# Moving the second tile's hybrid input projection ahead of the first expert gathers

## The reference, cut to what matters

```
h   = rms_norm(x, attn_norm)                     # h0, h1 for tile 0, 1
p   = h @ hyb_w_in                               # 1024 x 2760: the hybrid input projection
q,k,iq,ik of p are rotated (rope), iw picks keys, v stays
x  += attention(...) @ hyb_w_out                 # 16 heads: 8 with top-k selected keys, 8 plain
h   = rms_norm(x, ffn_norm)
q   = h @ w_q  (1024 x 2048)                     # then scores against 128 sub-keys, top 16 of each half,
expert, g = top-16 of the sums per head          # 8 heads, 16 experts each, chosen per token
x  += sum_k g_k * gelu(h . u_tab[expert_k]) * v_tab[expert_k]
```

## Time and profile before

| | us |
|---|---|
| median of 3 runs | 2119.39 (2116.23 to 2121.25) |
| the profiled execution's own time | 2126.27 |
| its span (first to last instruction) | 2124.5 |
| first gather starts (span time) | 560.49 |
| HBM read | 718.66 MB |

### The profile page before, as it was taken

The page is one execution under the profiler, slowest core; times in us unless marked ns, Lnnn a source line. Parts: engine busy times, 40 slices in busy tenths (PEclk is TensorE's granted clock), DMA queues, the critical chain, the costliest instruction groups (busy, mean ns, idle before and its releaser), DMA issues.

```text
span 2124.5 us, 15629 instructions
## 1 busy us (share of the span) xinstructions
PE 1621.2 (76%) x4546; PEld 816.7 (38%) x4546; DVE 1394.3 (66%) x3285; ACT 382.0 (18%) x886; POOL 1136.0 (53%) x1028
## 2 busy tenths in 40 slices
PE   3997999998555868988786788878668896566555
PEld 1465888444222434433343333334334442111111
DVE  6654342142798586588757668776684887777775
ACT  1022000012111022222222222221222221100001
POOL 0000000000376667677767767777687677777773
PEclk9976999998777979999897899999889999866888
DMA  9851468162699999999999999999999999999997
GB/s 357 294 200 60 159 198 325 54 240 79 235 370 327 401 397 387 402 404 408 401 401 401 405 403 405 406 376 402 397 367 379 406 397 369 407 410 409 409 409 311
DMA packets 254482, 720.78 MB, mean 339 GB/s; under 512 B 24518, under 2 KB 49598, under 8 KB 253886
## 3 DMA queue, kind: packets, MB, share of 16 engines
q0 software_dynamic: 147456, 536.94, 64.6%
q1 hardware_dynamic: 106942, 182.85, 24.0%
HBM read 718.66 MB, written 1.05 MB: 339 GB/s over the span
## 4 chain that ended last, share of the span: by engine, by line
PE 40%; DMA 22%; POOL 16%; DVE 12%; issue 7%; ACT 2%; SPq 1%; POOLq 0%; DVEq 0%; ACTq 0%
POOL gring L1699 16%; DMA gring<-in_peer_v_dram,sel_idx 15%; PE PS L621 12%; PE PS L753 7%; PE PS L825 5%; PE PS L826 5%; DMA gring<-in_peer_u_dram,sel_idx 4%; PE PS L727 4%; DVE gring L1537 3%; PE PS L566 3%; DMA wring<-in_hyb_w_in_dram 2%; DVE xs L1556 1%; PE PS L670 1%; PE PS L687 1%; PE PS L706 1%
## 5 line engine op out<-in xcount | busy, mean ns | idle before, releaser
L1699 POOL DMA_INDIRECT gring<-in_peer_u_dram,sel_idx x512 | 574.7, 1123 | 731.6 <-DVE sel_g L1523 560.0
L825 PE MATMUL PS<-gring,diags 128*128 128x512 f32 x704 | 426.6, 691 | 345.3 <-DMA gring<-in_peer_v_dram,sel_idx 217.3
L1699 POOL DMA_INDIRECT gring<-in_peer_v_dram,sel_idx x512 | 561.0, 1096 | 229.7 <-issue 126.7
L1537 DVE CUSTOM_DVE_ANT_0 gring<-gring,hs 128x1024 f32<-128x1024 f32 x400 | 482.5, 1222 | 142.9 <-DMA gring<-in_peer_u_dram,sel_idx 141.5
L621 PE MATMUL PS<-wring,hTs 128*128 128x512 f32 (+3 forms) x968 | 415.4, 580 | 20.2 <-DVE hTs L1125 8.3
L826 PE MATMUL PS<-gring,diags 128*128 128x512 f32 x704 | 413.5, 673 | 0.0
L825 PEld LDWEIGHTS PS<-gring,diags 128*128 128x128 f32 x704 | 126.7, 207 | 564.0 <-issue 412.5
L621 PEld LDWEIGHTS PS<-wring,hTs 128*128 128x128 f32 x968 | 180.8, 197 | 233.5 <-issue 226.0
L826 PEld LDWEIGHTS PS<-gring,diags 128*128 128x128 f32 x704 | 151.6, 215 | 199.2 <-issue 199.2
L1063 ACT ACTIVATE diags<-consts,acts 128x128 f32<-128x128 f32 x352 | 129.7, 396 | 482.4 <-PE PS L826 447.0
L1537 DVE CUSTOM_DVE_ANT_0 gring<-gring,PS 128x1024 f32<-128x1024 f32 x112 | 136.5, 1221 | 70.7 <-DMA gring<-in_peer_u_dram,sel_idx 70.7
(11 more groups left out here) (194 smaller groups left out, 1167.8 us busy)
## 6 DMA issues: line engine op xcount, KB each, us to landing
wring<-in_peer_w_q_dram SPq DMA_DIRECT2D x32, 1024.0 KB, 14.2
wring<-in_w_ada_dram SPq DMA_DIRECT2D x24, 1024.0 KB, 9.7
wring<-in_w_up_dram SPq DMA_DIRECT2D x44, 512.0 KB, 5.0
wring<-in_hyb_w_in_dram SPq DMA_DIRECT2D x20, 1024.0 KB, 7.8
wring<-in_w_in_dram SPq DMA_DIRECT2D x10, 1024.0 KB, 8.5
wring<-in_hyb_w_out_dram SPq DMA_DIRECT2D x8, 1024.0 KB, 21.5
gring<-in_peer_u_dram,sel_idx POOLq DMA_INDIRECT x512, 13.1
gring<-in_peer_v_dram,sel_idx POOLq DMA_INDIRECT x512, 13.6
```

Of the source, the lines that this page charges most:

```text
L825: pe.e.matmul(ybank[0], d, row[i % NG][:, 0:512], start=first, stop=last)
L1537: e.tensor_tensor_reduce(row[i % NG], row[i % NG], hbank if (l, t) == (1, 1) and hd else h[t], 1.0, 0.0, ALU.mult, ALU.add, acts[:, c:c + ...
L1699: gp.e.indirect_dma_start(out=row[i % NG], out_offset=None, in_=table, in_offset=bass.IndirectOffsetOnAxis(ap=sel_idx[:, c:c + 1], axis=0) ...
```

## The change

The end of tile 1's first block (`sq g1`, `norm g1`, `add g1`) and the norm of tile 1's h (`sq h1`, `norm h1`) move to just behind the first step of tile 0's `hyo`. h1's transposes are put behind the first step of `c00`; their result is written back into `h[1]` itself (in place), not into `hT`, and is the left operand of the projection. The seven column groups of `hyi` for tile 1 are put as follows: group 0 before the norm of `c00`; groups 1 to 4 behind pick parts 0 to 3 of group g = 0 (between the two `wq` steps of g = 1); group 5 behind pick part 4; group 6 behind `qturn` of g = 1 and the first `wq` step of g = 2. All seven are read out of PSUM by ScalarE as plain copies, the first six into `ahead`, a part of `keep`, and are not rotated there. The rotation is six new steps `hrope` on VectorE at the head of `hybrid(1)`, each counted as 1.5 units. `PACE[0]` becomes 251.4.

```diff
-PACE = (296.0, 216.3, 243.3)
+PACE = (251.4, 216.3, 243.3)
     def hybrid(t):
         if t:
-            put("sq", "h1")
-            yield 1.0
-            put("norm", "h1")
-        yield 3.0
-        put("hT", f"h{t}")
-        yield 1.0
-        put("hTe", f"h{t}")
-        yield 1.0
-        yield from projection(("hyi", t), (t,))
+            for c in range(6):
+                put("hrope", c)
+                yield 1.5
+        else:
+            put("hT", "h0")
+            put("hTe", "h0")
+            yield from projection(("hyi", 0), (0,))
         put("hqk", t)
...
+        if steps[-1] == ("mm", ("hyo", 0), (0,), 0, 0, 0):
+            put("sq", "g1")
+            put("norm", "g1")
+            put("add", "g1")
+            put("sq", "h1")
+            put("norm", "h1")
+
+    def hyi_ahead():
+        for c in range(7):
+            for k0 in (0, 4):
+                put("mm", ("hyi", 1), (1,), c, k0, 1)
+                if k0:
+                    put("evac", ("hyi", 1), c, 1)
+                yield
+
+    ahead = hyi_ahead()
     c00 = choose(0, 0)
-    while ("pick", 0, 0, 0, 5) not in steps:
+    next(c00)
+    put("hT", "h1")
+    put("hTe", "h1")
+    for _ in range(2):
+        next(ahead)
+    while ("qturn", 0, 0, 0) not in steps:
         next(c00)
-    put("sq", "g1")
-    while ("pick", 0, 0, 0, 6) not in steps:
+    while ("qturn", 0, 0, 1) not in steps:
         next(c00)
-    put("norm", "g1")
-    put("add", "g1")
+        if steps[-1][0] == "pick" and steps[-1][4] < 5:
+            for _ in zip(range(2), ahead):
+                pass
+    for _ in ahead:
+        pass
     together(16 + 32 * 7, PACE[0], c00, hybrid(1), choose(1, 0))
...
+        ahead = keep[:, 2816:5376]
...
-                        take(("mm", name, c, tl), "act" if name[0] == "wq" else "vec" if name[0] in (
+                        take(("mm", name, c, tl), "act" if name[0] == "wq" or name == ("hyi", 1) else "vec" if name[0] in (
...
+                if name[0] == "hyi" and c < 6:
+                    at, w = SPOTS[c0]
+                    last = copy(ahead[:, at:at + w], ps[:, 0:w])
+                    if c0 in (512, 1152):
+                        last = copy(val(t, 8) if c0 == 512 else iw[t], ps[:, 64:n])
+                    freed(key, last)
+                    return
...
+                    dst = hT[:, i0:i0 + 4, 0:128]
+                    if key == ("hT", "h1"):
+                        dst = h[1][:, 128 * i0:128 * i0 + 512].rearrange("p (b q) -> p b q", q=128)
...
+            def hrope(c):
+                c0 = PROJ["hyi"][1][c][0]
+                at, w = SPOTS[c0]
+                there(("mm", ("hyi", 1), c, 1))
+                r1, r2 = (work[:, 512 * (n % 6):512 * (n % 6) + 512] for n in (2 * c, 2 * c + 1))
+                dst = ahead[:, at:at + w]
+                heads = dst.rearrange("p (h w) -> p h w", w=64)
+                last, total = rope(heads, heads, 1, TR64, w // 64, r1, r2)
+                done(last)
+                so_far()
+                if w == 64:
+                    ve.wait_ge(*done(total()))
+                    e.tensor_copy(ahead[:, at + 64:at + 128], dst).then_inc(roped, 1)
+                else:
+                    total().then_inc(roped, 1)
```

More of the change, by code:

```diff
@@ L453, in program @@
             if s[0] == "evac" and (s[1][0], s[2]) == ("win", 3) or s[0] == "mrope" or (
-                    s[0] == "evac" and s[1][0] == "hyi" and s[2] < 6):
+                    s[0] == "evac" and s[1] == ("hyi", 0) and s[2] < 6) or s[0] == "hrope":
                 roped_n[s] = len(roped_n) + 1
@@ L594, in lhs_of @@
                     return lambda k: hT[:, 6 + k, cols]
+                if name == ("hyi", 1):
+                    return lambda k: h[1][:, 128 * k:128 * k + 128]
                 return lambda k: hT[:, k, cols]
@@ L762, in hqk @@
                 taken[2] = 4
-                pe.wait_ge(roped, roped_n[("evac", ("hyi", t), 5, t)])
-                turn(("hq", t), [pj[:, 128 * i:128 * i + 128] for i in range(12)])
-                turn(("hk", t), [pj[:, 1536 + 128 * i:1664 + 128 * i] for i in range(6)])
+                pe.wait_ge(roped, roped_n[("hrope", 5) if t else ("evac", ("hyi", 0), 5, 0)])
+                src = ahead if t else pj
+                turn(("hq", t), [src[:, 128 * i:128 * i + 128] for i in range(12)])
+                turn(("hk", t), [src[:, 1536 + 128 * i:1664 + 128 * i] for i in range(6)])
             def index(t):
@@ L869, in evac @@
                 key = ("mm", name, c, t)
-                if use[key][2] != me or name[0] in ("hyo", "mlo") or name[0] == "hyi" and c < 6:
+                if use[key][2] != me or name[0] in ("hyo", "mlo") or name == ("hyi", 0) and c < 6:
                     return
@@ L1124, in by_gain @@
                     ps = arrived((*key, i0))
+                    dst = hT[:, i0:i0 + 4, 0:128]
+                    if key == ("hT", "h1"):
+                        dst = h[1][:, 128 * i0:128 * i0 + 512].rearrange("p (b q) -> p b q", q=128)
                     freed((*key, i0), e.tensor_tensor(
-                        hT[:, i0:i0 + 4, 0:128], ps.rearrange("p (b q) -> p b q", q=128),
+                        dst, ps.rearrange("p (b q) -> p b q", q=128),
                         norm_cols[:, at + i0:at + i0 + 4].unsqueeze(2).to_broadcast([128, 4, 128]), ALU.mult))
@@ L1283, in evac @@
                     freed(key, e.tensor_tensor(xt, ps, xt, ALU.add))
-                elif name[0] == "hyi" and c < 6:
+                elif name == ("hyi", 0) and c < 6:
                     c0 = PROJ["hyi"][1][c][0]
@@ L1569, in vector_engine @@
                    "angles": angles, "score": score, "value": value, "fold": fold, "up": up, "gfold": gfold,
-                   "index": index, "mrope": mrope, "hold": hold, "u": dot, "gate": gate, "v": expert, "pick": pick}
+                   "index": index, "mrope": mrope, "hrope": hrope, "hold": hold, "u": dot, "gate": gate, "v": expert, "pick": pick}
             first = {"mod": modulate, "turn": attturn, "lin": mrope_key}
```

## The result

The changed kernel takes 2133.87 us (median of 4 runs, 2133.23 to 2136.03), the one before 2117.91 in the same job (4 runs, 2116.23 to 2121.25). The ratio is 1.0073, interval 1.0060 to 1.0085: slower by 16 us, where I forecast 11 us faster, and outside my range (2094 to 2126).

A forecast was written before the change was run, and what follows sets the result against it. The second half was taken as bound by bytes to fetch. First gather +20.1, bytes -23.1, idle DMA time -8: -11 us, 2115.3 from the profiled 2126.3, carried to 2108 against the median 2119.4; range 2094 to 2126.

The forecast's parts named there:

- How much later the first gather starts: Tile 0's first picks: exponential held on ScalarE behind copies of groups 1 to 5; first gather 580.6 for 560.5, +20.1 us.
- Bytes that leave: Tile 1's projection weights: 9.2 MB less to fetch behind the first gather, 23.1 us at 399 GB/s.
- The idle DMA time behind the first gather: Two stages, 115 us behind the first gather: 17.1 us of DMA time lost before; the change takes back a net 8 us.
- 3, 5 and 2: Behind the first gather, us taken back: loads in flight at the start 3, finish and norm gone 5, changed PACE 2.
- its bounds (-17 to +7): Idle DMA time behind the first gather: -17 with all of it back, +7 with nothing back and rotations in full.
- Rotations: Six rotations in one place behind the picks: 10.8 us of DVE, mostly covered by gathers in hand, 2 us lost.
- The 7.5 of my own working: At the rotations: DVE has 18.3 us of work for 10.8 of DMA, 7.5 us short if nothing is hidden.
- the 16 gathers in hand: At the rotations: POOL has up to 16 gathers (20 us) in hand, set against the 7.5 us shortfall.
- Rival 2: First 120 us of gathers: row ring without lead, POOL waits for dots, rotations unhidden (+7.5); slower, 2127 us; chance 0.21.
- Rival 4: At the rotations: two SBUF operands hold POOL's gathers, 7 us at most, 2115 us; chance 0.05.
- the finish of x and the norm that leave: Behind tile 0's choice: DVE's finish and ACT's square, table load and root leave; 5 of 7.9 us taken back.
- The further ScalarE copies: Copies of tile 1's projection out of PSUM: 6 at 0.6 us, beside a bound of bytes, cost nothing.

The follow-up runs named there:

- the edit: First choice's 256 dots made sums over the gathered row alone (one SBUF operand, product with h left out): on the changed kernel 1.0022, on the kernel before 0.9983.
- The changed kernels without the late start: Changed kernel with copies of groups 1 to 5 behind the exponential (also with dots, or rotations, moved), or those groups behind the second scores: 1.0029 to 1.0046.
- thin-weight: Kernel before, loading only 16 columns of each group of tile 1's projection weights: ratio 0.9960.
- early-norm: Kernel before with only the finish of x and the norm of tile 1 moved to hyo, projection left in place: ratio 0.9993.
- before (second profile): Kernel before, unchanged, profiled a second time as the yardstick: own time 2116.14 us.

## Why the prediction was wrong

- *How much later the first gather starts*: right in mechanism and nearly in size, +17.7 us counted from hyo's start (+18.4 in span time) for +20.1. More than half of the difference lies in front: PE took up the first w_q step 27.6 us behind hyo's start, where I had it at 28.9.
- *Bytes that leave*: right as bytes. The queue carried 18.10 MB between 505 and 575 us (forecast 18.6), and 7.3 MB for 9.2 were missing behind. Wrong as time, and this is the step that failed: "at 399 GB/s that is 23.1 us" takes every byte for bound, before and after. Before, 5.5 MB of the projection lay in the picks' stretch, which ran at 345 GB/s, and taking out 10.9 MB in place gained 8.5 us. After, the stretch that they left no longer runs at the bound (246 and 326 GB/s for 401 from 700 to 740 and to 820 us), and the 12 us made good from gather 100 to 120 only repay what the hole ahead of them cost.
- *The idle DMA time behind the first gather*: the picks' stretch gained 13.6 us where I took back 3, 5 and 2; by gathers it is 9 us without the rotations. That was right. But I looked for idle time only where before has it, up to 676 us. The 15.6 us from 700 to 740 and 15.1 from 740 to 820 were in neither my sum nor its bounds (-17 to +7).
- *Rotations*: "2 us lost" was 7 to 10. The 7.5 of my own working, with nothing hidden, was right; the 16 gathers in hand were no cover: POOL waited 2.1 us for DVE to free a row at 676 us, ahead of the first rotation at 682.5.
- *Rival 2* has the right place and sign, "the row ring has by then no lead, because DVE has been behind for 90 us", and its 2127 falls 7 us short: it still credits the 23 us of bytes.
- *Rival 4* was turned down by a row that says nothing on it. By the edit it is worth 11 to 12 us (7 when what the same edit gives the kernel before is taken off), where I had 7 at most, and it acts not at the rotations alone but at every dot with h in SBUF. It was there before the change too, at little or no cost (0.9983, up to 1.0000).
- *Small parts*: for the finish of x and the norm that leave I took 5 us back. Alone they bring 4.4 us by gather 80 (179.9 for 184.3), but nothing is left of it at gather 160, and the ratio, 0.9993, has 1 inside its interval. The further ScalarE copies I had at nothing; apart from the exponential, which I had counted, no run tests them alone.

What stays open: how the 15.6 us of the hole divide between PE's wait for the rotations, the indexer's latency and the order of dots on DVE. Leaving the rotations out fills part of it (280 GB/s from 700 to 740 for 246), moving five of them does not. The changed kernels without the late start are still 0.3 to 0.5% slower than before, and where they lose behind gather 256 is not explained either.

## What to carry to other kernels

Before you price bytes at the bound's rate, count where they land: here 3.3 of 10.9 MB lay in stretches at that rate. Then ask what such a stretch would run at without them. Here a projection stood between two chains of VectorE, with the DMA engines full beside it; with the projection moved away, they stood partly idle. Before a row is used against a contention, check that its operands lie in the same memories as those in question.

## What was unexpected of the hardware

- An indirect gather of 0.94 us on POOL takes up to 2.0 us when it starts beside a DVE operation with two SBUF operands, as if it waited for its end, and two engines can lock in that step for 20 us. Beside dots with one operand in PSUM it stays at 0.94 (193 of 193).
- The kernel before took 2118, 2159 and 2167 us in jobs on different chips. More than half of the difference between the first two arises where gathers alone run: the thin-weight and early-norm edits of it, on the chip with 2159, move 369 and 372 GB/s from 1700 to 1960 us and 381 and 386 from there to 2080, before (second profile) on the chip with 2118 moves 396 and 409.
